# A hybrid layer on one core: the decay matrix and the scaling of the probabilities made by ScalarE, the solution scaled from PSUM

## The reference

```python
s_own = jnp.where(key_pos[None, :] <= t[:, None], q @ k.T * scale, -jnp.inf)
p = softmax(s_own)                       # pr: exponentials, then times 1 / their sum
out = p @ v

g = cumsum(g)                            # log decays
decay = jnp.where(incl, jnp.exp(g[:, None] - g[None, :]), 0.0)
lower = jnp.where(strict, (k * beta) @ k.T * decay, 0.0)
sol = triangular_solve(lower + eye, [v * beta, ...])
```

## Time and profile before

| | |
|---|---|
| runs shown | 1334.96, 1335.96, 1341.8 us |
| the profiled execution | 1340.07 us, its span 1338.0 us |
| busy share of the span | PE 85%, VectorE 55%, GpSimd 48%, ScalarE 36% |
| mean granted clock of PE | 0.945 |
| chain that ended last | PE 41%, DMA 36%, VectorE 7% |

### The profile page before, as it was taken

One profiled execution on the slowest core, in us unless ns is written; L12 is line 12 of the kernel. 1 busy time (PEld: TensorE's weight loads), 2 busy tenths in 40 slices (PEclk: granted clock), 3 DMA queues, 4 the chain that ended last, 5 costly groups with the idle time before them and its releaser, 6 DMA issues.

```text
span 1338.0 us, 16698 instructions
## 1 busy us (share of the span) xinstructions
PE 1140.7 (85%) x5387; PEld 793.8 (59%) x5387; DVE 735.6 (55%) x1648; ACT 478.0 (36%) x889; POOL 646.8 (48%) x452
## 2 busy tenths in 40 slices
PE   5788999889989999999689879788788887977877
PEld 4667898889888889896444435344343443522332
DVE  3324656665664322232496666665656666666553
ACT  4453555445444676641131222212212122221211
POOL 3665645665466466572335344344534444434430
PEclk8899999999999999999789899889898999999899
DMA  6444334242333445493499999999999999999993
GB/s 212 111 129 124 97 91 110 78 125 79 93 92 98 110 126 142 132 323 96 161 412 418 415 421 418 418 421 415 422 417 419 421 422 422 422 421 422 421 422 125
DMA packets 168381, 355.28 MB, mean 266 GB/s; under 512 B 7959, under 2 KB 131214, under 8 KB 135438
## 3 DMA queue, kind: packets, MB, share of 16 engines
q0 software_dynamic: 36864, 268.45, 48.4%
q1 hardware_dynamic: 131470, 86.27, 22.2%
HBM read 353.64 MB, written 1.05 MB: 265 GB/s over the span
## 4 chain that ended last, share of the span: by engine, by line
PE 41%; DMA 36%; DVE 7%; issue 6%; ACT 5%; POOL 3%; SPq 0%; DVEq 0%; POOLq 0%; ACTq 0%
DMA top<-peer_uv_dram,route 18%; DMA scratch<-peer_uv_dram,route 11%; PE ps L1692 9%; PE ps L1361 6%; PE ps L1362 6%; PE ps L1363 6%; DMA gate_part<-peer_uv_dram,route 4%; PE ps L1658 3%; POOL split L863 3%; PE ps L1515 2%; ACT split L543 2%; DMA front<-in_w_branch_dram 2%; PE ps L1642 2%; PE ps L1534 1%; DVE rest L997 1%
## 5 line engine op out<-in xcount | busy, mean ns | idle before, releaser
L863 POOL TENSOR_TENSOR split<-front,split 128x1024 fp32r<-128x1024 f32 x128 | 309.9, 2431 | 213.7 <-ACT split L543 213.5
L1692 PE MATMUL ps<-top 128*128 128x512 f32 x448 | 218.7, 643 | 53.6 <-ACT top L819 53.6
L1361 PE MATMUL ps<-split 128*128 128x256 f32 (+1 forms) x768 | 244.4, 318 | 17.8 <-POOL split L863 12.4
L1362 PE MATMUL ps<-split 128*128 128x256 f32 (+1 forms) x768 | 227.9, 297 | 0.0
L1363 PE MATMUL ps<-split 128*128 128x256 f32 (+1 forms) x768 | 227.6, 296 | 0.0
L912 POOL DMA_INDIRECT top<-peer_uv_dram,route x112 | 128.3, 1145 | 163.1 <-PE ps L1692 144.7
L543 ACT ACTIVATE split<-front 128x1024 fp32r<-128x1024 f32 x128 | 133.4, 1056 | 203.8 <-PE ps L1363 147.4
L1692 PEld LDWEIGHTS ps<-top 128*128 128x128 f32 x448 | 90.1, 206 | 174.6 <-issue 104.5
L1241 DVE CUSTOM_DVE_ANT_0 top<-top,scratch 128x1024 f32<-128x1024 f32 x112 | 137.2, 1225 | 81.9 <-DMA top<-peer_uv_dram,route 81.9
L1361 PEld LDWEIGHTS ps<-split 128*128 128x128 f32 x768 | 150.5, 196 | 25.1 <-POOL split L863 9.5
L1362 PEld LDWEIGHTS ps<-split 128*128 128x128 f32 x768 | 150.6, 196 | 3.5 <-issue 0.5
(11 more groups left out here) (261 smaller groups left out, 1920.7 us busy)
## 6 DMA issues: line engine op xcount, KB each, us to landing
front<-in_w_in_dram SPq DMA_DIRECT2D x88, 512.0 KB, 3.8
front<-in_w_branch_dram SPq DMA_DIRECT2D x24, 512.0 KB, 5.0
front<-in_w_mem_kv_dram SPq DMA_DIRECT2D x16, 512.0 KB, 4.2
branch_part<-in_peer_w_q_dram SPq DMA_DIRECT2D x8, 1024.0 KB, 25.9
top<-in_w_out_dram SPq DMA_DIRECT2D x8, 512.0 KB, 6.3
top<-peer_uv_dram,route POOLq DMA_INDIRECT x112, 26.1
cst<-constants_dram SPq DMA_DIRECT2D x1, 1544.5 KB, 9.6
scratch<-in_x_dram SPq DMA_DIRECT2D x2, 512.0 KB, 3.9
```

What stands on the lines that cost most here:

```text
L863: pool.tensor_tensor(halves[i % 3][:, 1], raw[i % 3], halves[i % 3][:, 0], ALU.subtract).then_inc(lo_ready, 1)
L1361: pe.matmul(dst, lhs[0], rhs[0], start=first, stop=False)
L1362: pe.matmul(dst, lhs[0], rhs[1], start=False, stop=False)
L1692: ins = pe.matmul(ps[:, 2 * c + half, :], diag[:, k % 8, :], rows_uv[k][:, D + half * 512:D + (half + 1) * 512], start=False, stop=last an ...
```

## The change

ScalarE gets two new functions. `log_decays(h + 1)` is called in its head behind `evacuate_dv(h + 1)`, and `log_decays(0)` in the lead behind the first convolution, after a wait for the gates. `normalise(h)` is called behind high(4) and waits for VectorE's reciprocal. The same work is taken out of VectorE's levels 1 and 2 and its lead; VectorE keeps the reciprocal. vn's first half is taken from PSUM instead of the copy, ahead of the wait for `cross` instead of behind `w1_ready`.

```diff
@@ ScalarE
+            def log_decays(h):
+                g0, g1 = (small[:, bass.ds(h + (120 + 8 * c), 1)] for c in range(NC))
+                act.activation(Gm[:, 0:T], upto[:, 0:T], ACT.Copy, scale=g0)
+                act.activation(Gm[:, T:384], upto[:, T:384], ACT.Copy, scale=g1).then_inc(names["Gm_ready"].sem, 1)
+
+            def normalise(h):
+                on(act, "psums", h)
+                act.activation(pr[:, 0:P], pr[:, 0:P], ACT.Copy, scale=mx[:, 6:7])
+                act.activation(pr[:, P:384], pr[:, P:384], ACT.Copy, scale=mx[:, 7:8]).then_inc(names["pnorm"].sem, 1)
...
             evacuate_conv(0, ("lead", 0), 1)
+            act.wait_ge(s_gate, 11)
+            log_decays(0)
             high("lead", 0, 4)
...
                 high(*tile(4))
+                normalise(h)
...
                 high(*tile(5))
                 if not last:
                     evacuate_dv(h + 1, kind, 2)
+                    log_decays(h + 1)
@@ VectorE
-            def log_decays(h):
-                g0, g1 = (small[:, bass.ds(h + (120 + 8 * c), 1)] for c in range(NC))
-                dve.tensor_scalar(Gm[:, 0:T], upto[:, 0:T], g0, None, ALU.mult)
-                dve.tensor_scalar(Gm[:, T:384], upto[:, T:384], g1, None, ALU.mult).then_inc(done("Gm_ready"), 1)
...
                         dve.reciprocal(mx[:, 6:8], mx[:, 4:6]).then_inc(done("psums"), 1)
-                        on(dve, "psums", h)
-                        dve.tensor_scalar(pr[:, 0:P], pr[:, 0:P], mx[:, 6:7], None, ALU.mult)
-                        dve.tensor_scalar(pr[:, P:384], pr[:, P:384], mx[:, 7:8], None, ALU.mult).then_inc(done("pnorm"), 1)
-                    if s == 2 and not last:
-                        log_decays(h + 1)
...
                 dve.tensor_copy(vp[:, 0:P], ps[:, 4, 0:P]).then_inc(done("vp0"), 1)
+                dve.tensor_scalar(vn[:, 0:P], ps[:, 4, 0:P], b0, None, ALU.mult)
                 on(dve, "cross", h)
                 dve.tensor_tensor(w1, dv[:, P:T], ps[:, 3, 0:P], ALU.subtract).then_inc(done("w1_ready"), 1)
-                dve.tensor_scalar(vn[:, 0:P], vp[:, 0:P], b0, None, ALU.mult)
...
-            log_decays(0)
```

## The result

The changed kernel takes 1322.32 us (median of four runs, 1321.69 to 1323.54), the kernel before beside it 1337.88 (1334.96 to 1341.8). The ratio is 0.9875, with a 95% interval from 0.9853 to 0.9898. The profiled execution took 1321.69 us; its span is 1319.6 against 1338.0, 18.4 us less. The forecast was 1317.5 us, and 18.3 us less by the profiled execution. The median of the kernel before is 1.9 us above that of the forecast, because a fourth run (1339.8 us) has joined the three.

What follows compares the result with a forecast made beforehand. PE bounds the eight heads, with its waits and clock. Old losses of 31.4 us less new ones of 13.1 give 18.3 us: 1340.07 to 1321.8 profiled, 1317.5 from the 1335.96 median; range 1309 to 1329.

Steps and rivals of the forecast that it cites:

- (a): Level 2: log_decays leaves VectorE, so PE's 3.04 and 0.85 us waits go; level 4 then costs 7 x 0.33 = 2.3 us.
- waits of 3.04 us: PE's waits ahead of level 3 in heads 1, 3, 4, 5 and 6, put down to VectorE's subtraction; forecast to go.
- level 4's 0.33: PE's wait ahead of level 4, seen in head 2, forecast to stand in all seven heads: 2.3 us lost.
- (c): Level 1: normalise behind high(4) on ScalarE makes PE wait 1.35 us at the transposes, 10.8 us over 8 heads; 0.67 goes.
- price of 1.3 us for the low clock: Heads: time lost to the 1.2 GHz level after a 3.04 us wait, also charged after the last head's 1.95 us.
- (b): log_decays on ScalarE behind evacuate_dv, two ACTIVATEs of 0.41 and 0.32 us: costs nothing, covered by PE's own tile work.
- old wait of the last head: Last head: PE's 1.95 us wait, counted with 1.3 us of clock among the 31.4 us the old kernel loses.
- (d): vn's first half read from PSUM, one instruction earlier: nothing; at most 2.8 us of loss or 5.6 us of gain.
- the rival's doubt: Rival: the clock falls at the new 1.35 us wait, 10.4 us come back over eight heads, 1328; chance 0.13.
- The collision did not move on: Rival: L1088 and L1089 also wait for GpSimd's L863, PE's 3 us stay; 1342 at most, chance 0.07.
- The landing of tile 4's weights: Rival, slower: high(4) waits for late weights, delaying normalise behind it on ScalarE; 1356 at 3.5 us late, chance 0.04.
- my answer to it: Against the VectorE-is-faster rule: L996's median of 2577 ns next to GpSimd decides for moving (a) and (c) to ScalarE.

## Why the prediction was right, and where it was not

*What bounds the heads.* Right. PE with its waits and its clock gave the sum, 18.3 us against 18.4 in the span, and the heads alone give 18.4 (343.9 and 325.5). That the tenth is met is luck in part: 10.0 + 2.4 us of the forecast waits were measured and not 13.1, and 0.7 us that nobody forecast stand ahead of level 1 in head 0. Behind the heads nothing changed by as much as 0.1 us in all.

*(a) The log decays.* The waits of 3.04 us went, level 4's 0.33 came in all seven heads (0.32 measured), and the clock stayed up. But the step took for granted that log_decays must leave VectorE for that. With it on VectorE and the probabilities moved, the time is the same, 1320.72; with it at level 6 and nothing moved, it is 1316.44. The collision depended on 0.8 us of timing, which (c) alone changes. The forecast costed (a) and (c) as independent; either of them removes the 3 us waits. The price of 1.3 us for the low clock behind each of them held in the profiled execution, where all five have it; one of the six of the execution at 1345.46 us had none.

*(b) Its arrival on ScalarE.* Costed at nothing, and no wait of PE points to it. With the log decays back on VectorE and out of GpSimd's way the distance of two heads is the same, 40.53 us, so their place on ScalarE costs nothing.

*(c) The probabilities.* Right in place and size: 1.35 us forecast, 1.29 measured in seven heads and 1.00 in the last, where 0.16 us of waiting ahead of level 2 stand beside it. The forecast head of 40.7 us takes 40.55. The old wait of the last head, 1.95 us and 1.3 for the clock, was struck from the sum without a reason, although the landing behind it stays. The trace has the reason: between the reciprocal (421.30 before, 404.88 after) and the subtractions stood the two scalings, 1.4 us of VectorE's time, and without them PE waits 0.16 us there.

*(d) vn.* Right: nothing, by its own run.

*The range.* Its lower end was added up wrongly: the three terms given for it, 3, 5.6 and 1.3 us, lead from 1317.5 to 1307.6 and not to 1309. The measured time lies far from that end.

*From the profiled execution to the median.* This step failed, by 4.8 us. The sum gave 1321.8 us for the profiled execution, and 1321.69 was measured. I then took the full 18.3 us from a median that lay 4.1 us lower. Of the 4.8 us, 1.9 are that the median of before itself rose to 1337.88 with a fourth run; the other 2.9 are that the medians differ by 15.6 us and not by 18.3, and the rounding to 1317.5. But the kernel before has executions with more and with fewer hit heads (six and 1345 us were seen, 1331.6 is its fastest time), the changed one spreads over 1.9 us only. The probable reading is that runs of before below 1340 had fewer collisions and so less to gain; an execution near 1335 was not profiled, so that it is not shown.

*The rivals.* The clock did not fall at 1.29 us. It did once in seven at 2.0 us, so the rival's doubt was sound and its price of 1.3 us a head was near (1.5 measured). The collision did not move on to L1093 and L1094, which take 0.42 and 0.41 us. The landing of tile 4's weights did not come late in any head; that of tile 3's did in the last head, as before, and PE waited 0.16 us ahead of level 2. The rule that VectorE, where it has a performance mode, is the faster engine for what both can do (the Trainium skill, Perfetto Trace Analysis, Optimizing Scalar/DVE Operations) turned out better than my answer to it: 0.48 and 0.28 us on VectorE at level 6 against 0.50 and 0.39 us for L591 and L592 on ScalarE, and 1316.44 us against 1322.32. What spoke against it was the place of the instruction, not the engine.

## What to carry to other kernels

When an instruction takes 2.5 us that once took 0.35, look at what runs on the other engine when it is issued, and try another place in its own queue before another engine. When work goes to an engine with a queue in order, put it where its input is ready, ahead of an instruction that waits for something later: here two lines exchanged were worth 11 to 14 us by the medians (12 to 13 in the heads), nearly as much as the change. And a saving that was counted in one execution belongs to that execution: where what collides differs from one to the next, as it did here between five and six heads, it can't be taken whole from a median.

## What the runs showed of the hardware that was not expected

Among GpSimd's short products (0.7 us each) VectorE's scaling of 256 columns took 0.34 us, as if alone, and the one of 128 columns behind it 0.75 instead of 0.28. Issued just ahead of a 2.4 us low half or at its start it took 2.35 to 2.58 us in most heads (0.35 in head 2); issued near the end of one it took 0.39 us (head 0 of the kernel before) and 0.48 (level 6). So it waits for what is left of the low half.

The clock did not follow the length of PE's wait. Waits of 2.0 us in seven heads were followed once by the 1.2 GHz level and six times not, waits of 2.32 us four times of six, waits of 3.04 us in the kernel before sixteen times of seventeen; after 1.95 us it fell in the kernel before and not in the one with the probabilities back on VectorE.

And the kernel before spread over 14 us in one set of seven runs (1331.6 to 1345.3), though over 7 only in another of fifteen; the two kernels in which only the probabilities' scaling still collides over 7, the changed one over 2, with four runs each. That makes the collisions a likely source of the spread, which is not shown; the kernel with log_decays pushed into the way spread over 4 us only in ten runs, so a collision that is hit every time would be steady.
